# Attention of a hybrid layer: three transposed groups set between score blocks on TensorE, and split on VectorE ahead of the row maximum

## What is computed

```python
s = jnp.einsum("bqhd,bkhd->bhqk", qn, k_nope) + jnp.einsum("bqhr,bkr->bhqk", qr, k_rope)
p = jax.nn.softmax(s.astype(jnp.float32) * scale, axis=-1).astype(v.dtype)
return jnp.einsum("bhqk,bkhd->bqhd", p, v)
```

## Time and profile before

| what | value |
|---|---|
| median of three executions | 1846.21 us (1843.69 to 1848.38) |
| the profiled execution | 1846.43 us, with a span of 1844.6 us from first to last instruction |
| PE, PEld | 1694.6 us (92%), 1510.1 us (82%) of the span |
| DVE, ACT | 1050.7 us (57%), 714.9 us (39%) |
| mean granted TensorE clock | 0.973 of full speed |
| units of attention | from 550.53 us (first score matmul) to about 859 us |

### The profile page before, as it was taken

One profiled execution on the slowest core, in us unless ns is written; L12 is line 12 of the kernel. 1 busy time (PEld: TensorE's weight loads), 2 busy tenths in 40 slices (PEclk: granted clock), 3 DMA queues, 4 the chain that ended last, 5 costly groups with the idle time before them and its releaser, 6 DMA issues. The chain is left out here.

```text
span 1844.6 us, 24583 instructions
## 1 busy us (share of the span) xinstructions
PE 1694.6 (92%) x9795; PEld 1510.1 (82%) x9795; DVE 1050.7 (57%) x1584; ACT 714.9 (39%) x1183; POOL 78.7 (4%) x116
## 2 busy tenths in 40 slices
PE   5799999999769889996998899999999999899997
PEld 5687888877657777875877899999999999788885
DVE  6645755328745454444556655555555555366787
ACT  5543322333344343344454433333333333434453
POOL 1000000004300000000000000000000000000000
PEclk8899999989989999998998999999999999999999
DMA  8433142000230000002531122222222223763345
GB/s 306 139 102 126 64 167 94 25 1 20 53 137 18 1 12 1 1 1 97 188 115 46 61 82 96 96 96 97 79 84 95 90 90 112 236 221 120 122 133 202
DMA packets 90226, 176.32 MB, mean 96 GB/s; under 512 B 9825, under 2 KB 43313, under 8 KB 90113
## 3 DMA queue, kind: packets, MB, share of 16 engines
q1 hardware_dynamic: 86016, 169.75, 27.0%
q0 software_dynamic: 4096, 5.01, 0.9%
HBM read 131.02 MB, written 43.70 MB: 95 GB/s over the span
## 5 line engine op out<-in xcount | busy, mean ns | idle before, releaser
L418 PE MATMUL psF<-gv,gu_ring 128*128 128x320 f32 x1232 | 384.5, 312 | 15.3 <-DVE gv L2286 5.3
L420 PE MATMUL psF<-gv,gu_ring 128*128 128x320 f32 x1232 | 383.8, 311 | 0.0
L419 PE MATMUL psF<-gv,gu_ring 128*128 128x320 f32 x1232 | 383.7, 311 | 0.0
L418 PEld LDWEIGHTS psF<-gv,gu_ring 128*128 128x128 f32 x1232 | 234.3, 190 | 16.7 <-issue 12.2
L419 PEld LDWEIGHTS psF<-gv,gu_ring 128*128 128x128 f32 x1232 | 234.2, 190 | 0.0
L420 PEld LDWEIGHTS psF<-gv,gu_ring 128*128 128x128 f32 x1232 | 234.0, 190 | 0.0
L418 PE MATMUL psF<-d_w_ring,d_hid_ring 128*128 128x512 f32 x360 | 140.9, 391 | 6.2 <-DVE d_w_ring L2375 6.1
L419 PE MATMUL psF<-d_w_ring,d_hid_ring 128*128 128x512 f32 x360 | 140.8, 391 | 0.0
L420 PE MATMUL psF<-d_w_ring,d_hid_ring 128*128 128x512 f32 x360 | 140.7, 391 | 0.0
L418 PE MATMUL psP<-hT_hi,win_hi 128*128 128x512 f32 (+1 forms) x336 | 120.9, 360 | 0.7 <-DVEq L991 0.7
L419 PE MATMUL psP<-hT_lo,win_hi 128*128 128x512 f32 (+1 forms) x336 | 119.5, 356 | 0.0
(11 more groups left out here) (385 smaller groups left out, 3638.2 us busy)
## 6 DMA issues: line engine op xcount, KB each, us to landing
hid_variants<-hraw SPq DMA_DIRECT2D x77, 320.0 KB, 2.2
d_hid<-hid_variants SPq DMA_DIRECT2D x77, 320.0 KB, 3.0
m_wring<-in_w_mod SPq DMA_DIRECT2D x24, 1024.0 KB, 7.0
d_b<-in_w_down SPq DMA_DIRECT2D x44, 256.0 KB, 3.8
win_raw<-in_w_in SPq DMA_DIRECT2D x18, 512.0 KB, 4.6
raw_gu<-in_w_gate SPq DMA_DIRECT2D x11, 512.0 KB, 4.1
raw_gu<-in_w_up SPq DMA_DIRECT2D x11, 512.0 KB, 4.9
hraw<-in_w_gate SPq DMA_DIRECT2D x11, 512.0 KB, 3.8
```

Source lines behind the costliest of these rows:

```text
L418: pe.matmul(out, w_hi, x_hi, start=first, stop=False, skip_group_check=onto)
L419: pe.matmul(out, w_hi, x_lo, start=False, stop=False, skip_group_check=onto)
L420: return pe.matmul(out, w_lo, x_hi, start=False, stop=last, skip_group_check=onto)
```

## The change

In every slot with t of 2 or more, PE's order becomes: values part 1 (even slots), first group, first score block of 512, second group, second score block of 512, third group, values part 0 (odd slots), and the score block of 256 at the end. A prompt unit's only score block also stands at the end. On DVE the product at L1564 comes first in even slots, then `pt_lo` of all three groups, and then the maximum. The conditions of each wait stay as they were, ACT's queue is unchanged, and no instruction is added or removed.

```diff
--- before.py
+++ after.py
@@ -1564,15 +1564,14 @@
                 dve.tensor_tensor(L.mixA[:, h, t * P:(t + 2) * P], psO[:, 0:2 * P], rb[:], ALU.mult
                                   ).then_inc(o_read, 1)
 
-            def pt(u, part):
+            def pt(u):
 
                 g0, r = n_groups(u), (u % 2) * P
                 for i, g in enumerate(groups(units[u][1])):
-                    if (i >= 2) == bool(part):
-                        dve.wait_ge(pth_ready, g0 + i + 1)
-                        dve.tensor_tensor(pt_lo[:, g[0]:g[-1] + 1, r:r + P], psPT[:, (g0 + i) % 2, 0:len(g), :],
-                                          pt_hi[:, g[0]:g[-1] + 1, r:r + P].bitcast(F32), ALU.subtract
-                                          ).then_inc(ptl_ready, 1)
+                    dve.wait_ge(pth_ready, g0 + i + 1)
+                    dve.tensor_tensor(pt_lo[:, g[0]:g[-1] + 1, r:r + P], psPT[:, (g0 + i) % 2, 0:len(g), :],
+                                      pt_hi[:, g[0]:g[-1] + 1, r:r + P].bitcast(F32), ALU.subtract
+                                      ).then_inc(ptl_ready, 1)
 
             def split_in(first, last):
                 for i in range(first, last):
@@ -1590,13 +1589,11 @@
             for h in range(HEADS):
                 for t in range(NT):
                     u = h * NT + t
-                    if t >= 2:
-                        pt(u - 2, 0)
                     if t % 2 == 0 and t >= 4:
                         out(u // 2 - 2)
+                    if t >= 2:
+                        pt(u - 2)
                     maximum(u)
-                    if t >= 2:
-                        pt(u - 2, 1)
                     if t >= 1:
                         invert(u - 1)
                     if t == 5 and h + 1 < HEADS:
@@ -1605,12 +1602,10 @@
                     rotate(h + 1)
                 invert(u)
                 out(u // 2 - 1)
-                for part in range(2):
-                    pt(u - 1, part)
+                pt(u - 1)
                 if h + 1 < HEADS:
                     low(h + 1, "k")
-                for part in range(2):
-                    pt(u, part)
+                pt(u)
                 if h + 1 < HEADS:
                     low(h + 1, "fold")
                 out(u // 2)
@@ -1650,20 +1645,19 @@
                                         x_lo[:, k, c0:c0 + w], k == 0, k == kn - 1)
                     mm.then_inc(proj, 1)
 
-            def scores(u, part):
-
-                t, shared = units[u][1], pieces(u)[-1:]
-                if len(pieces(u)) == 1 and u % 2 == 0:
-                    shared = []
-                todo = shared if part else pieces(u)[:len(pieces(u)) - len(shared)]
+            def scores(u, piece):
+
+                t = units[u][1]
+                last = piece == len(pieces(u)) - 1
+                late = last and not (len(pieces(u)) == 1 and u % 2 == 0)
                 if u == 0:
                     pe.wait_ge(in_lo, len(landed))
-                if u % NT == 0 and part == 0:
+                if u % NT == 0 and piece == 0:
                     pe.wait_ge(drained, n_proj(units[u][0] + 1))
-                elif u % NT >= 1 + (part == 0):
-                    pe.wait_ge(e_ready, u - 1 + part)
+                elif u % NT >= 1 + (not late):
+                    pe.wait_ge(e_ready, u - 1 + late)
                 q = slice(t * P, (t + 1) * P)
-                for col, k0, w in todo:
+                for col, k0, w in pieces(u)[piece:piece + 1]:
                     out, ks = S[:, col:col + w], slice(k0, k0 + w)
                     pe.matmul(out, q_hi[:, q], kn_hi[:, ks], start=True, stop=False)
                     pe.matmul(out, q_hi[:, q], kn_lo[:, ks], start=False, stop=False)
@@ -1671,15 +1665,15 @@
 
                     pe.matmul(out, qr[:, q], L.kr_hi[:, ks], start=False, stop=False)
                     mm = pe.matmul(out, qr[:, q], L.kr_lo[:, ks], start=False, stop=True)
-                    if (col, k0, w) == pieces(u)[-1]:
+                    if last:
                         mm.then_inc(score, 1)
 
-            def transposes(u, part):
+            def transposes(u, group=None):
 
                 g0 = n_groups(u)
                 pe.wait_ge(e_ready, u + 1)
                 for i, g in enumerate(groups(units[u][1])):
-                    if (i >= 2) != bool(part):
+                    if group not in (None, i):
                         continue
                     if g0 + i >= 2:
                         pe.wait_ge(ptl_ready, g0 + i - 1)
@@ -1718,25 +1712,24 @@
             for h in range(HEADS):
                 for t in range(NT):
                     u = h * NT + t
-                    scores(u, 0)
+                    n = len(pieces(u))
                     if t % 2 == 0 and t >= 4:
                         values(u // 2 - 2, 1)
-                    if t >= 2:
-                        transposes(u - 2, 0)
-                    scores(u, 1)
-                    if t >= 2:
-                        transposes(u - 2, 1)
+                    for i in range(3):
+                        if t >= 2:
+                            transposes(u - 2, i)
+                        if i < n - 1:
+                            scores(u, i)
                     if t >= 3 and t % 2 == 1:
                         values(u // 2 - 1, 0)
+                    scores(u, n - 1)
                 if h + 1 < HEADS:
                     project(h + 1, "qrope")
                 values(u // 2 - 1, 1)
-                for part in range(2):
-                    transposes(u - 1, part)
+                transposes(u - 1)
                 if h + 1 < HEADS:
                     project(h + 1, "k")
-                for part in range(2):
-                    transposes(u, part)
+                transposes(u)
                 if h + 1 < HEADS:
                     project(h + 1, "fold")
                 for part in range(2):
```

## The result

| | before | after |
|---|---|---|
| median | 1846.21 us (5 executions, 1843.69 to 1848.38) | 1856.88 us (5 executions, 1854.09 to 1859.40) |
| ratio | | 1.0056, 95% interval 1.0043 to 1.0069 |
| profiled execution, its span | 1846.43 us, 1844.6 us | 1854.09 us, 1852.3 us |
| attention: start of the first score matmul to start of the last product (L1564) | 550.53 to 859.39: 308.86 us | 549.74 to 868.33: 318.59 us |

The change makes the kernel 10.7 us slower by the medians. The profiled execution happens to be the fastest of the five; its span is 7.7 us longer, its attention 9.7 us. The 2 us between these come from outside: before attention 0.79 us less, behind it 983.94 instead of 985.22, with the same code.

The account below looks back on a forecast made before the run. Queue order in a loop through PE, DVE and ACT was taken to bound attention. Slot terms gave +2.75 in heads 0 and 2, +3.44 in head 1, +1.60 in head 3: +10.5, near 1856.7 us; range 1852 to 1862.

Parts of the forecast that it names:

- t = 2: Slot 2 of each head: same wait on the chain, no values; 5.68 us against 4.86, +0.82.
- t = 6 with the split: Slot 6, heads 0 to 2: DVE's weights' split delays the third group; 7.92 us, -1.14, or -0.45 in head 1.
- t = 8: Slot 8 of each head: three groups with no scores between; maximum at 6.06 us against 7.60, -1.54.
- t = 9: Slot 9 of each head: values and scores follow the third group at 2.57; 5.04 us against 2.93, +2.11.
- The odd slots, +2.10: Slots 3, 5, 7: PE waits 1.50 us before the third group, values and block of 256 behind; 6.95 us against 4.85.
- The even slots, -2.29: Slots 4 and 6 with values part 1: chain hidden, third group not delayed; 6.77 us against 9.06.
- the edges: Costs outside the plain pair of odd and even slots: the weight split and slots 2, 8 and 9.
- Unknown costs: Attention: extra group turns -0.4 to +1.1 us, chain intervals +-1, clock -1.7 to +5; none taken for the forecast.
- The waits simply go: Rival at odd slots' third group: PE never stops, 5.45 us instead of 6.95, about 1827 us in all; chance 0.04.
- The edges are hidden: Rival: plain pair nearly cancels, weight split and slots 2, 8, 9 cost nothing more; 1844 to 1850 us; chance 0.07.
- The clock is kept: Rival in head 2: score block of slot 8 prevents the clock's fall, 1.7 us come back, 1855.0 us; chance 0.12.
- The clock falls more often: Rival: new 1.5 us waits beside transposes bring two to four more falls; 1860 to 1864 us; chance 0.10.

Follow-up runs that it names:

- the fourth experiment: Changed kernel with groups and score blocks still alternating, but the block of 256 ahead of the third group and the maximum ahead of that group's pt_lo: 1844.52 us.
- second and third experiment: Second: kernel before with DVE's new order and PE's old one, 1855.36 us. Third: changed kernel with the block of 256 ahead of values part 0, 1851.17 us.
- the fifth: Kernel before, with only the product at L1564 moved ahead of the groups' pt_lo on DVE in even slots: 1842.32 us.
- The third experiment: Changed kernel with the score block of 256 put ahead of values part 0 in odd slots on PE: 1851.17 us.
- the first experiment: Changed kernel's PE order with DVE's order of before, the maximum ahead of the third group's pt_lo: 1889.72 us.
- the split in slot 4: Changed kernel with the weights' split on ACT and DVE in slot 4 instead of slot 5: 1867.85 us.

## Why the prediction was right

**The forecast** was 1856.7, measured are 1856.88; part of that closeness is luck, as an execution varies by 2 us. In the profiles attention is 9.73 us longer, or 10.8 with the low clock before set aside (below), against 10.54 forecast. The steps behind it can be checked one by one, since attention repeats them. From maximum to maximum, forecast and measured in us:

| step | before | forecast | after |
|---|---|---|---|
| t = 2 | 4.86 | 5.68 | 5.69 |
| odd, t = 3, 5, 7 | 4.85 | 6.95 | 6.94 to 6.96 (two of 12 at 7.05) |
| even, t = 4, and 6 in head 3 | 9.06 | 6.77 | 6.77 |
| t = 6 with the split | 9.06 | 7.92 | 8.02 |
| the same in head 1 | 9.07 | 8.61 | 8.62 |
| t = 8 | 7.61 | 6.06 | 5.97 |
| t = 9 | 2.93 | 5.04 | 5.03 (5.07 and 5.13 once each) |
| last maximum to the next head's first | 26.43 | 24.92 | 24.92 |

By heads the changed kernel is 2.79, 3.48, 1.69 and 1.77 us longer; forecast were 2.75, 3.44, 2.75 and 1.60. The range is less well founded than the steps: the bounds that are named (-0.4 and +1.1, 1 either way, -1.7 and +5) add up to 1853.6 and 1863.8, not to 1852 and 1862. The measured time lies in both.

**The odd slots, +2.10.** Shown by two sides. Work taken out of the loop shortens them by its own length (two tiles: 0.72; the block of 256 ahead of all four: 1.27, less than 1.50 because then DVE's third group decides, as in slot t = 2). Work put ahead of the wait costs nothing (13.8 us of it, hidden).

**The even slots, -2.29, and the edges.** Measured as forecast. At t = 8 I took the reciprocals' copy at its whole duration of 0.38; the next instruction starts 0.26 us after it (601.45 to 601.71), so 0.10 was too much. Behind the split 0.10 was missing: the product starts 0.15 us after the split's end (588.94 to 589.09), where I had counted nothing. Over the kernel they cancel nearly.

**Unknown costs.** More groups between score blocks cost nothing (the fourth experiment). The clock I left out of the forecast. Head 2 is where that is seen: 1.69 instead of 2.75, because the fall of the clock that the earlier trace rows show did not come back, in this head or any other. It was worth 0.28 + 0.78 = 1.06 us (the steps 3.21 and 27.21 us before against 2.93 and 26.43 of head 0), not the 1.7 that half of 3.4 us gives. That term was too large for two reasons. Matmuls with 256 columns came 0.21 us apart instead of 0.12, which is less than double. And in the same place of head 0 PE waits 0.32 us, which the slower matmuls of head 2 fill; the first line is of head 0, the second of head 2:

```profile
605.52 0.41 PE L1687 MATMUL psPT<-const,prob 128*128 128x128 f32 x2 [0.32 <-DVE pt_lo L1573]
...
772.04 0.63 PE L1687 MATMUL psPT<-const,prob 128*128 128x128 f32 x2
```

**The rivals.** *The waits simply go*: no, at the third group the chain came at 4.48 us and PE at 3.01. *The edges are hidden*: no, they cost what was worked out. *The clock is kept* happened beside the forecast in this one profile: attention shows no low clock at all. Its reason is not shown. The clock fell about slot t = 8 in one head of four in the profile before and in two of four in the second and third experiment, and in none in the fifth, which has PE's order of before. The stretch ahead of the fall has the same busy time in the heads that kept the clock; the earlier trace rows have it for head 2 alone, and this is head 0:

```profile
600.10:604.40 4.30, 2.52 (x21) 1.87 (x19) 2.51 (x7) 2.65 (x7) 0.00 (x0) 1.00 0.00 0
```

The third experiment has the score block of t = 8 between the groups of unit 6 and those of unit 7, as the changed kernel does, and the clock fell all the same, so this block alone does not decide. What does stays open. *The clock falls more often*: not in the changed kernel's profile, whose waits in odd slots are 1.5 us; but longer waits can bring it, as the first experiment (2.10 us) and the split in slot 4 (3.46 us) show.

## What to carry to other kernels

Where engines have queues in program order, follow one unit round the loop and write down, behind each wait, what else is queued there: the price of a wait is what stands behind it, not its length. A reordering that lowers the number of stalls (39 to 27) can lengthen the loop; counting stalls would have got the sign wrong here, while a few intervals read from the timeline gave every step to 0.1 us. And parts of a losing change can win alone (interleaving -3 us, the product first -5.5 us), so try them one at a time. Their gains and costs need not add up: in even steps these two take away the same 0.33 us.

## What the runs showed of the hardware

Long waits on PE can cost more than themselves. With PE busy 1.04 of 3.5 us, the granted clock then fell to 0.50 for 6.8 us, and 10 needless matmuls inside each of three such waits made the kernel about 7 us faster. With PE busy 2.30 of 4.40 us (the first experiment) it fell as well, at seven places of attention; but behind the other five of its 12 waits of 2.10 us it did not, and no kernel was run against that one. In the changed kernel PE waited 1.5 us in every odd slot, and its granted clock was 1.00 over the whole of attention:

```profile
549.74:868.33 318.59, 270.92 (x1746) 234.71 (x1746) 155.37 (x292) 124.17 (x244) 0.00 (x0) 1.00 0.02 5
```

The Trainium skill, in "TensorE: Matmul & The Clock Gate", section "HAM oscillation — how this bites in real kernels", tells of a kernel in which a wait between two bursts of matmuls lowers the clock, so that the next burst starts cold. The kernel with the split in slot 4 agrees with it: 3.46 us of waiting, then a granted clock of 0.50.
